# Seven products of half blocks for the feed-forward up units 4 to 15 of a two-block float32 network

## What is computed

```python
def _sq_relu_mlp(h, w1, w2):
    return jnp.square(jax.nn.relu(h @ w1)) @ w2
...
        h2 = _rms_norm(x, norm_mlp[l]) * (1.0 + sc2) + sh2
        x = x + g2 * _sq_relu_mlp(h2, w_mlp1[l], w_mlp2[l])
...
    return _rms_norm(x, norm_final)
```

## Time and profile before

| | |
|---|---|
| median of 3 runs | 1625.81 us |
| the profiled execution, its own time | 1626.04 us |
| its span, first to last instruction | 1624.3 us |
| TensorE (PE) busy | 1607.9 us, 99% of the span |
| TensorE weight loads (PEld) busy | 1336.6 us, 82% |
| VectorE (DVE) busy | 829.1 us, 51% |
| ScalarE (ACT) busy | 680.8 us, 42% |
| GpSimd (POOL) busy | 583.0 us, 36% |
| granted TensorE clock, mean | 0.999 |

### The profile page before, as it was taken

One profiled execution on the slowest core, in us unless ns is written; L12 is line 12 of the kernel. 1 busy time (PEld: TensorE's weight loads), 2 busy tenths in 40 slices (PEclk: granted clock), 3 DMA queues, 4 the chain that ended last, 5 costly groups with the idle time before them and its releaser, 6 DMA issues.

```text
span 1624.3 us, 20270 instructions
## 1 busy us (share of the span) xinstructions
PE 1607.9 (99%) x8308; PEld 1336.6 (82%) x8308; DVE 829.1 (51%) x1239; ACT 680.8 (42%) x1043; POOL 583.0 (36%) x289
## 2 busy tenths in 40 slices
PE   9999999999999999999999999999999999999998
PEld 6888898889888878888887767789878788888887
DVE  7787867676665364443443646681356621111112
ACT  6533343443432433555455463423435643332323
POOL 1002113221344434334333434353323465555542
PEclk9999999999999999999999999999999999999999
DMA  6453333343355223233223241122112133222221
GB/s 234 153 204 131 125 127 134 116 132 121 133 205 207 104 91 104 93 103 103 94 90 121 78 156 66 52 87 73 53 40 78 65 117 104 91 103 92 98 85 52
DMA packets 53252, 179.16 MB, mean 110 GB/s; under 512 B 6428, under 2 KB 7068, under 8 KB 52776
## 3 DMA queue, kind: packets, MB, share of 16 engines
q1 hardware_dynamic: 53160, 177.88, 31.5%
HBM read 172.58 MB, written 2.12 MB: 108 GB/s over the span
## 4 chain that ended last, share of the span: by engine, by line
PE 92%; DVE 5%; ACT 1%; issue 1%; DMA 0%; SPq 0%; POOL 0%; DVEq 0%; ACTq 0%; POOLq 0%
PE banks L427 90%; PE banks L430 2%; DVE ACC L1182 1%; DVE wl L1146 1%; ACT T L1969 0%; DMA maskf<-cst_dram 0%; DVE ada L1130 0%; DVE X L1130 0%; ACT wh L1972 0%; ACT Sc L1969 0%; DVE ML L1130 0%; DVE T L1912 0%; ACT L1969 0%; DVE Sc L1130 0%; DVE E L1912 0%
## 5 line engine op out<-in xcount | busy, mean ns | idle before, releaser
L2553 POOL TENSOR_TENSOR wl<-raw,wh 128x1024 fp32r<-128x1024 f32 x171 | 424.2, 2485 | 525.3 <-ACT wh L1972 525.3
L427 PE MATMUL banks<-HH,wh 128*128 128x512 f32 (+1 forms) x1040 | 413.2, 397 | 2.6 <-ACT T L1969 0.9
L427 PE MATMUL banks<-HL,wh 128*128 128x512 f32 (+1 forms) x1040 | 402.3, 390 | 0.3 <-DVE HL L1130 0.3
L1972 ACT ACTIVATE wh<-raw 128x1024 fp32r<-128x1024 f32 x246 | 257.0, 1052 | 296.9 <-PE banks L427 289.0
L427 PE MATMUL banks<-HH,wl 128*128 128x512 f32 x1032 | 282.6, 390 | 0.0
L427 PEld LDWEIGHTS banks<-HH,wh 128*128 128x128 f32 (+1 forms) x1040 | 194.9, 187 | 50.0 <-issue 5.5
L427 PEld LDWEIGHTS banks<-HL,wh 128*128 128x128 f32 (+1 forms) x1040 | 194.7, 187 | 42.0 <-issue 1.4
L427 PEld LDWEIGHTS banks<-HH,wl 128*128 128x128 f32 x1032 | 193.4, 188 | 41.5 <-issue 1.0
L427 PE MATMUL banks<-wh,HH 128*128 128x256 f32 x448 | 128.5, 287 | 0.0
L427 PE MATMUL banks<-wl,HH 128*128 128x256 f32 x448 | 126.7, 283 | 0.0
L427 PE MATMUL banks<-wh,HL 128*128 128x256 f32 x448 | 126.6, 283 | 0.0
(11 more groups left out here) (354 smaller groups left out, 2627.5 us busy)
## 6 DMA issues: line engine op xcount, KB each, us to landing
raw<-wst_dram SPq DMA_DIRECT2D x294, 512.0 KB, 3.2
X<-xT_dram SPq DMA_DIRECT2D x8, 512.0 KB, 6.6
CB<-sums_dram SPq DMA_DIRECT2D x12, 256.0 KB, 3.1
D<-dec_dram SPq DMA_DIRECT2D x12, 256.0 KB, 2.8
out_dram<-XT SPq DMA_DIRECT2D x8, 256.0 KB
QS<-QX SPq DMA_DIRECT2D x24, 64.0 KB, 2.6
KSw<-KX SPq DMA_DIRECT2D x24, 64.0 KB, 2.0
MX<-memT_dram SPq DMA_DIRECT2D x2, 512.0 KB, 8.7
```

Of the source, the lines that this page charges most:

```text
L427: return pe.eng.matmul(dst, w, x, start=start, stop=stop, skip_group_check=True)
L1972: return eng.activation(dst, src, ACT.Copy)
L2553: tt(wl[:, q, :], raw[:, i % NRAW, :], wh[:, q, :].bitcast(F32), ALU.subtract).then_inc(*by_pool("low", u))
```

## The change

The up units 4 to 15 (`SEVEN = 4`) are computed by a scheme that multiplies two matrices cut in 2 by 2 blocks with seven block products instead of eight. A tile of weights (512 input rows by 256 columns) and the matching input (512 by 512 tokens) are so cut; each block product has 128 output features, 256 input rows (two blocks of 128, `q`) and 256 tokens. So TensorE issues 7 x 2 x 3 = 42 products of 256 columns per tile instead of 24 of 512, in banks 2 to 5.

What the scheme adds: four sums of weight blocks per tile of kind "s" (VectorE, three `tensor_tensor` over 512, 256 and 256 columns into `WS`), their high half `SH_` (ScalarE, 1024 columns) and their low half `SL_` (GpSimd, 1024 columns). The same for the input, once: `x_whole` puts `HH` and `HL` together again in `XW` (GpSimd, 8 of 512 columns), `x_sums` adds (VectorE, 4 of 512 columns for each half `kh`), `x_sums_high` (ScalarE, 2 of 1024 each) and `x_sums_low` (VectorE, 2 of 1024 each). After a unit of seven products ScalarE copies one product out, VectorE puts the results together in four additions from PSUM, and applies relu and square in one instruction (`hidden`).

The groups of hidden features have 512 instead of 1024, and the order (`FF`) is: up, down, down, up, down, down, with a down unit of a single tile that reads four hidden blocks; each of the 32 down tiles now adds its own two banks to `X`, where before two tiles shared them. `FHI` and `FLO` are half as large. From group 2 on GpSimd makes all the low halves `FLO` (the change's title calls these output weights; which engine makes the low halves `wl` of the weight tiles stays as it was). The SP queue reloads the buffer of an "s" tile only after its sums.

The core of the diff (removed code, the same loops in the old grouping, is mostly left out):

```diff
+FF = [("up", 0), ("up", 1)]
+for _g in range(1, 8):
+    for _h in range(2):
+        FF += [("up", 2 * _g + _h), ("down", _g - 1, 2 * _h), ("down", _g - 1, 2 * _h + 1)]
+FF += [("down", 7, _n) for _n in range(4)]
+SEVEN = 4
...
+    for step in FF:
+        if step[0] == "up":
+            pair("up", 0, 8, (256 * step[1],), "s" if step[1] >= SEVEN else "w")
+        else:
+            pair("down", 4 * step[1], 4 * step[1] + 4, (256 * step[2],))
...
+NS = 3
...
+        def seven(u):
+            for kh in range(2):
+                w = feed.take()
+                high, low = blocks(wh[:, w % NW, :]), blocks(wl[:, w % NW, :])
+                sums = [s[:, S_AT[w] % NS, :].rearrange("p (s q c) -> p s q c", s=4, q=2) for s in (SH_, SL_)]
+                def of_w(j, i):
+                    return high[:, j, :, i, :], low[:, j, :, i, :]
+                def of_s(n):
+                    return sums[0][:, n, :, :], sums[1][:, n, :, :]
+                def of_x(j, h):
+                    return [x[:, 4 * kh + 2 * j:4 * kh + 2 * j + 2, 256 * h:256 * h + 256] for x in (HH, HL)]
+                def of_t(n):
+                    return XSH[:, kh, n, :, :], XSL[:, kh, n, :, :]
+                def product(b, c, a, x):
+                    o, s0 = bank[b][:, 256 * c:256 * c + 256], kh == 0 and c == 0
+                    for q in range(2):
+                        mm(o, a[0][:, q, :], x[0][:, q, :], s0 and q == 0, False)
+                        mm(o, a[0][:, q, :], x[1][:, q, :], False, False)
+                    for q in range(2):
+                        i = mm(o, a[1][:, q, :], x[0][:, q, :], False, kh == 1 and q == 1)
+                    return i
+                pe.wait_ge(done("high", w), done("low", w), done("x sums", kh), *free[2])
+                product(2, 0, of_w(1, 0), of_x(1, 0))
+                product(2, 1, of_w(0, 0), of_x(0, 0)).then_inc(*by_pe("seven", u, kh, 0))
+                pe.wait_ge(done("sums high", w), done("sums low", w), *free[3])
+                product(3, 0, of_w(1, 1), of_t(3))
+                product(3, 1, of_s(2), of_t(1)).then_inc(*by_pe("seven", u, kh, 1))
+                pe.wait_ge(*free[4])
+                product(4, 0, of_s(1), of_t(0))
+                product(4, 1, of_s(0), of_t(2)).then_inc(*by_pe("seven", u, kh, 2))
+                pe.wait_ge(*free[5])
+                product(5, 0, of_s(3), of_x(1, 1)).then_inc(*by_pe("seven", u, kh, 3))
+                by_pe.also("w free", w)
+            for b in range(2, 6):
+                free[b] = tuple(done("kept", ("up", u), j) for j in range(2))
+        def up(u):
+            if u >= SEVEN:
+                seven(u)
+            else:
+                unit_f(("up", u), (2, 3) if u == 1 else (0, 1), *hi_lo("x4"), by_k=2 if u == 1 else 0)
+        def down(g, n):
+            u = feed.take()
+            pe.wait_ge(*(done("l", "f", g, k) for k in range(4)))
+            features(("down", g, n), FHI[g % 2], FLO[g % 2], range(4), True, True, (0, 1), u)
+        for step in FF[1:]:
+            (up if step[0] == "up" else down)(*step[1:])
...
+            if PLAN[i][0] == "s":
+                v = S_AT[u]
+                w, s = blocks(raw[:, i % NRAW, :]), WS[:, v % 2, :].rearrange("p (s q c) -> p s q c", s=4, q=2)
+                dve.wait_ge(done("raw", i), done("sums low", S_TILES[v - 2]) if v > 1 else done("l", "f", 0, 1))
+                tt(s[:, 0:2, :, :], w[:, 0, :, :, :].rearrange("p q i c -> p i q c"), w[:, :, :, 1, :],
+                   ALU.subtract).then_inc(*by_dve())
+                dve.wait_ge(by_dve.last())
+                tt(s[:, 2, :, :], w[:, 1, :, 1, :], s[:, 0, :, :], ALU.add).then_inc(*by_dve())
+                dve.wait_ge(by_dve.last())
+                tt(s[:, 3, :, :], w[:, 1, :, 0, :], s[:, 2, :, :], ALU.subtract).then_inc(*by_dve("summed", i))
...
+        def x_sums(kh):
+            x = XW[:, 4 * kh:4 * kh + 4, :].rearrange("p (j q) (h c) -> p j q h c", q=2, c=256)
+            b11, b12, b21, b22 = (x[:, j, :, h, :] for j in range(2) for h in range(2))
+            dve.wait_ge(*(done("x whole", k) for k in range(4 * kh, 4 * kh + 4)), done("l", "f", 0, 1),
+                        done("x sums", kh - 1) if kh else None)
+            tt(XS[0][:, 0, :, :], b12, b11, ALU.subtract).then_inc(*by_dve())
+            stt(XS[1][:, 0, :, :], b22, -1.0, b12, ALU.mult, ALU.subtract).then_inc(*by_dve())
+            dve.wait_ge(by_dve.last())
+            tt(XS[0][:, 1, :, :], b22, XS[0][:, 0, :, :], ALU.add).then_inc(*by_dve("x summed", kh, 0))
+            dve.wait_ge(by_dve.last())
+            tt(XS[1][:, 1, :, :], b21, XS[0][:, 1, :, :], ALU.subtract).then_inc(*by_dve("x summed", kh, 1))
+        def x_sums_low(kh):
+            for n in range(2):
+                dve.wait_ge(done("x sums high", kh, n), done("x summed", kh, 1))
+                tt(XSL[:, kh, 2 * n:2 * n + 2, :, :], XS[n][:, :, :, :], XSH[:, kh, 2 * n:2 * n + 2, :, :].bitcast(F32),
+                   ALU.subtract).then_inc(*by_dve("x sums", kh))
+        def seven(u):
+            g, n = u // 2, 2 * (u % 2)
+            kept = done("kept", ("up", u - 1), 0) if u > SEVEN else None
+            dve.wait_ge(done("seven", u, 1, 1), done("first product", u), kept)
+            tt(PS[:, 1, :], bank[3][:, 256:512], PS[:, 0, :], ALU.add).then_inc(*by_dve())
+            dve.wait_ge(done("seven", u, 1, 2), by_dve.last())
+            tt(PS[:, 2:4, :], psum[:, 4, :].rearrange("p (a c) -> p a c", a=2), PS[:, 1:2, :].to_broadcast([128, 2, 256]),
+               ALU.add).then_inc(*by_dve())
+            t = turn("hidden", g, n + 1)
+            dve.wait_ge(by_dve.last(), temp_free("hidden", g, n + 1))
+            tt(t[:, :].rearrange("p (a c) -> p a c", a=2), psum[:, 3:5, 0:256], PS[:, 3:4, :].to_broadcast([128, 2, 256]),
+               ALU.add).then_inc(*by_dve("kept", ("up", u), 1))
+            hidden(g, n + 1, t)
+            t = turn("hidden", g, n)
+            dve.wait_ge(done("seven", u, 1, 3), temp_free("hidden", g, n))
+            tt(t[:, :].rearrange("p (a c) -> p a c", a=2), psum[:, 2:6:3, 0:256], PS[:, 0:3:2, :],
+               ALU.add).then_inc(*by_dve("kept", ("up", u), 0))
+            hidden(g, n, t)
+        def hidden(g, k, t):
+            dve.wait_ge(by_dve.last())
+            stt(t[:, :], t[:, :], 0.0, t[:, :], ALU.max, ALU.mult).then_inc(*by_dve("f", g, k))
+        def up(u):
+            feed.unit()
+            if u >= SEVEN:
+                seven(u)
+                return
+            g = u // 2
+            for j in range(2):
+                k = 2 * (u % 2) + j
+                t = turn("hidden", g, k)
+                square(g, k, t)
+                if made[0] % 3 == 0:
+                    temp_used("hidden", g, k)
+            if u == 1:
                 for j in range(2):
...
+                    square(g, j, E[j])
+            if u == 2:
+                x_sums(0)
+            if u == 3:
+                x_sums_low(1)
+        def down(g, n):
+            feed.take()
+            for j in range(2):
+                t = 2 * n + j
+                dve.wait_ge(done("unit", ("down", g, n), j), done("kept", ("down", g - 1, n), j) if g else None)
+                if g == 7 and t == 7:
+                    for h in range(2):
+                        c = slice(256 * h, 256 * h + 256)
+                        stt(X[:, t, c], bank[j][:, c], mod[:, 40 + t:41 + t], X[:, t, c], ALU.mult, ALU.add).then_inc(*by_dve("last tile", h))
+                    by_dve.also("kept", ("down", g, n), j)
+                    turn("last", "x5")
+                    continue
+                stt(X[:, t, :], bank[j], mod[:, 40 + t:41 + t], X[:, t, :], ALU.mult, ALU.add).then_inc(*by_dve("kept", ("down", g, n), j))
+                if g == 7:
+                    add_square("x5", t, T, t == 0, t == 6, free=done("sum", "x3"))
+            if (g, n) == (0, 0):
+                x_sums_low(0)
+            if (g, n) == (0, 1):
+                x_sums(1)
...
+            if PLAN[i][0] == "s":
+                v = S_AT[u]
+                act.wait_ge(done("summed", i), done("w free", S_TILES[v - NS]) if v >= NS else None)
+                copy(SH_[:, v % NS, :], WS[:, v % 2, :]).then_inc(*by_act("sums high", u))
...
+        def x_sums_high(kh):
+            for n in range(2):
+                act.wait_ge(done("x summed", kh, n))
+                copy(XSH[:, kh, 2 * n:2 * n + 2, :, :], XS[n][:, :, :, :]).then_inc(*by_act("x sums high", kh, n))
...
+            if u >= SEVEN:
+                act.wait_ge(done("seven", u, 1, 0), done("kept", ("up", u - 1), 0) if u > SEVEN else done("x sums", 1))
+                copy(PS[:, 0, :], bank[2][:, 256:512]).then_inc(*by_act("first product", u))
+                for k in (2 * (u % 2) + 1, 2 * (u % 2)):
+                    high(g, k, temp("hidden", g, k))
+                return
...
+                pool.wait_ge(done("sums high", u))
```

(62 more changed lines are left out.)

123 lines of the change are left out of this document (46 added, 77 removed).

## The result

The changed kernel takes 1697.88 us (median of 4 runs, 1696.34 to 1698.97) against 1625.83 for the kernel before (4 runs). The ratio is 1.0443, with an interval of 1.043 to 1.0456: 72 us slower. The profiled execution took 1698.65 us, its span is 1696.8, 72.5 us more than before.

The account below looks back on a forecast made before the run. PE, 99% busy, was taken to bound the kernel by number of products times spacing. From 1626.0 us: -10.0 products, +20.1 start, +49.5 periods, +7 clock, +66.6 in all, giving 1692 us, range 1645 to 1720.

Parts of the forecast that it names:

- The products: Up units of seven: 84 products spaced 0.1196 us take 10.05 instead of 10.88 us; twelve units save 10.0 us.
- That rival: Sevens take longer than 84 x 0.1196 us, say by weight loads not hidden; at most a few us, no chance given.
- Who may run beside whom: VectorE instructions with both operands in SBUF and GpSimd `tensor_tensor` exclude each other for whole instructions; the other's waiting one goes next.
- The period: One seven and two down tiles: second down tile waits 4.5 us for X<-banks behind the sums, 11 times, 49.5 us.
- the race: Rival: first FLO gets the port before the second `hidden`; stops of 2.2 instead of 4.5 us, 1663 us; chance 0.25.
- The start: Before and around the first seven, input preparation delays wl and X: 6.5, 4.5, 0.8 and 8.3 us, together 20.1 us.
- The clock: After PE's new stops the granted clock may fall to 1.2 GHz: 0.5 us for each of 14, 7 us.
- No turns: Rival: VectorE keeps the port through a run of sums; no stops in steady periods, start costs 13, 1629 us; chance 0.14.
- wholly hidden: Rival: additions and input preparation are hidden wholly by idle VectorE and GpSimd; only -10.0 us remains, 1616 us; chance 0.06.
- The clock rival: After each stop a whole down tile runs at half rate, 76 us, up to 1761 us; chance 0.10 for above 1720.
- Small or nothing: `x_sums(1)`, ScalarE's copies, DMA, SP's and VectorE's added waits, TensorE's new waits and the kernel's end cost little or nothing.

Follow-up runs that it names:

- the run with the PSUM operand: Changed kernel with a PSUM bank as second operand of VectorE's three sums per s tile, block sums left out of the result: 1632.38 us, one run.
- X first: Changed kernel, but in the first down tile after each up unit VectorE adds to X before making the next weight sums: 1639.39 us, ratio 1.0086.
- the kernel with two bank pairs: Changed kernel in its own order, but every second down unit uses banks 6 and 7 instead of 0 and 1: 1662.02 us, ratio 1.0229.

## Why the prediction held, point by point

The forecast was 1692 us with a range of 1645 to 1720; 1697.9 was measured.

**The products** were right: in the sevens they start 0.12 us apart (1383.24, 1383.36, 1383.48), also with the new stationary tiles. That rival falls.

**Who may run beside whom** was right. It was read from three places of the kernel before where the turns show and one with a PSUM operand where they don't; the run with the PSUM operand settles it.

**The period** was right step by step. After the end of a seven, forecast and measured: the second `hidden` starts at 2.3 and 2.26, the first FLO at 2.35 and 2.37, the first sum ends at 4.8 and 4.65, the second at 6.4 and 6.1, the third at 9.1 and 8.55, X's first half at 9.85 and 9.2. The stop is 3.9 instead of 4.5 (each change of turn took less than I gave it), eleven times: 43 instead of 49.5. `hidden` was ahead of FLO by 0.11 us in this period, so **the race** went as forecast; the same stop eleven times (3.89 to 3.92) says that it is no chance. That there is such an order at all was the largest open point, and one row pair carried it.

**The start** was sized too high: 13.5 us were measured and 20.1 forecast. The step that failed is X of tile (0,0) behind the first `x_sums`: I gave 4.5 us and it was 1.2. The sums ended at 1310.6 where I wrote 1313.1, and the tile itself ended 0.7 later than I wrote, on the low clock. The last stop was 6.7 instead of 8.3, the wl behind four `x_whole` 5.6 instead of 6.5, and the 0.8 us at up unit 3 did not come.

**The clock** was sized too low: 25.4 us were measured and 7 forecast. I took 0.5 us per stop because a stop of 4.5 hardly exceeded the 3.0 us that the end of the kernel shows. It was 1.5 to 2.6 us at 12 of 13 long stops, 2.1 on average. The two wrong sizes, 13 too much for stops and 18 too little for the clock, nearly cancel. So the total came near partly by luck, though the mechanisms are the ones forecast.

**Rivals.** "No turns" (1629) and "wholly hidden" (1616) fall by the traces; the kernels with X first and the PSUM operand come near 1629 because there the turns no longer matter, not because there are none. The clock rival (above 1720) was right in kind, but its price of 76 us was three times what came.

**Small or nothing**: right. No wait for DMA or for SP's added wait ended an idle time of PE, and the order alone cost 1.2 us of stop, for which the forecast had no term.

## What to carry to other kernels

Where PE is 99% busy, ask of added helper work not how many microseconds it is but which engine's next instruction it stands in front of: here 1.5 us of sums, put before an addition that frees a PSUM bank, cost 3.9 us of stop and about 2 of clock. When VectorE works on SBUF operands beside a busy GpSimd, price each instruction at its own length plus one whole GpSimd instruction, as long as one is waiting each time, and prefer few long ones or an operand in PSUM. Start a new scheme only after its preparation has had slack to run in, and count with each stop of TensorE what the clock may take after it: here 25 us on top of 56.

## What the runs showed of the hardware that was not expected

Stops of the same length, 3.9 us, meet the fall of the granted clock at different moments. In the stop that ends at 1393.33 the clock is full, and it is at half from about 1394.5 to 1397.9. In the one that ends at 1419.95 it is at half from about 1418.4, while TensorE stands still, until 1425.2. Over the long stops the fall came 8 times in the stop and 4 times up to 1.2 us after it. For the stops of 3.9 us it cost about 2.5 us in the first case and 1.6 in the second, and once of eleven nothing. What decides between these is open.

Shorter stops can have it too. In the kernel with two bank pairs, whose stops are of 2.0 us, some periods take 23.1 us and others 24.6 (period by period from 1421.58: 1444.66, 1469.24, 1492.32, 1516.93); four of the ten stops from 1398 us on have low clock behind them, 1.5 us each. The stops of 0.8 us in the kernel with the additions first never had it.

The turns go by whole instructions in both directions: in the first down tile of a period, VectorE's dependent sums, with 0.03 us between them, never kept the port when a GpSimd instruction stood waiting, in all eleven periods (1.78 to 1.79, 1.39 to 1.40 and 2.45 us each time). What decides if both become ready at once was not tried.
